# Attention of a hybrid decoder layer: from one head at a time to pairs of heads on the two halves of the array

## What is computed

```python
# stick-breaking head
z = q @ k.T * scale                       # causal: s < t
log_keep = where(causal, -softplus(z), 0)
tail = cumsum(log_keep, reverse=True) - log_keep
a = where(causal, exp(log_sigmoid(z) + tail), 0);  y = a @ v
# MoBA head (own block only)
s = where(t >= s, q @ k.T * scale + bias[bucket(t - s)], -inf);  y = softmax(s) @ v
# layer
h = x + (sigmoid(g_sb) * (y_sb @ w_proj_sb) + sigmoid(g_mb) * (y_mb @ w_proj_moba)) @ w_out
h = h + MoE(rmsnorm(h));  out = rmsnorm(h) * norm_final_g
```

## Time and profile before

| | |
|---|---|
| median of 3 runs | 1309.89 us (1307.11 to 1310.67) |
| span of the profiled execution, first to last instruction | 1304.8 us |
| TensorE busy | 1151.2 us (88%) |
| VectorE, ScalarE, GpSimd busy | 207.3, 210.2, 18.6 us |
| chain that ended last | TensorE 88%, VectorE 7%, ScalarE 4% |
| attention stage, first scores to first L901 | 54.8 to 190.3 us of the span |

### The profile page before, as it was taken

One profiled execution on the slowest core, in us unless ns is written; L12 is line 12 of the kernel. 1 busy time (PEld: TensorE's weight loads), 2 busy tenths in 40 slices (PEclk: granted clock), 3 DMA queues, 4 the chain that ended last, 5 costly groups with the idle time before them and its releaser, 6 DMA issues.

```text
span 1304.8 us, 15767 instructions
## 1 busy us (share of the span) xinstructions
PE 1151.2 (88%) x6100; PEld 472.1 (36%) x6100; DVE 207.3 (16%) x424; ACT 210.2 (16%) x356; POOL 18.6 (1%) x68
## 2 busy tenths in 40 slices
PE   7999999878888888888888888888888888888884
PEld 6675444433333333333333333333333333333331
DVE  1301222231111111111111111111111111111112
ACT  2363230211111111111111111111111111111111
POOL 1010000000000000000000000000000000000000
PEclk9999999979899989999998999899989998999897
DMA  9913324339999999999999999999999999999970
GB/s 336 354 65 129 128 85 160 147 113 386 399 399 397 398 401 393 395 405 401 396 400 395 393 395 395 409 397 387 399 402 397 396 403 403 405 394 399 401 308 33
DMA packets 86624, 437.04 MB, mean 335 GB/s; under 512 B 7704, under 2 KB 7760, under 8 KB 53744
## 3 DMA queue, kind: packets, MB, share of 16 engines
q1 hardware_dynamic: 84880, 434.19, 83.8%
q10 hardware_dynamic: 1424, 1.57, 0.5%
q0 software_dynamic: 304, 1.06, 0.2%
HBM read 435.74 MB, written 1.06 MB: 335 GB/s over the span
## 4 chain that ended last, share of the span: by engine, by line
PE 88%; DVE 7%; ACT 4%; issue 1%; DMA 0%; DVEq 0%; SPq 0%; ACTq 0%
PE bank L984 35%; PE bank L1010 22%; PE bank L818 6%; PE bank L958 5%; PE bank L815 4%; PE bank L949 4%; PE bank L901 2%; PE bank L912 2%; DVE gates L758 2%; DVE gates L760 2%; DVE gates L754 2%; PE bank L1001 2%; ACT gates L545 2%; ACT gates L547 1%; PE bank L978 1%
## 5 line engine op out<-in xcount | busy, mean ns | idle before, releaser
L984 PE MATMUL bank<-ring,gates 128*64 128x512 f32 x2048 | 460.1, 596 | 0.0
L1010 PE MATMUL bank<-ring,gates 128*64 128x512 f32 x1024 | 286.9, 724 | 22.0 <-ACT gates L547 22.0
L984 PEld LDWEIGHTS bank<-ring,gates 128*64 128x64 f32 x2048 | 140.9, 137 | 252.1 <-issue 244.9
L754 DVE TENSOR_SCALAR gates<-bank 128x512 f32<-128x512 f32 x32 | 22.1, 691 | 862.0 <-PE bank L984 862.0
L1010 PEld LDWEIGHTS bank<-ring,gates 128*64 128x64 f32 x1024 | 84.0, 166 | 205.3 <-issue 174.7
L1001 PE MATMUL bank<-ident,gates 128*128 128x128 f32 x128 | 21.1, 289 | 95.9 <-DVE gates L760 95.9
L818 PE MATMUL bank<-ring,colsT 128*128 128x512 f32 x192 | 85.0, 596 | 0.0
L545 ACT ACTIVATE gates<-gates 128x512 f32<-128x512 f32 x32 | 20.1, 629 | 398.7 <-DVE gates L754 398.7
L958 PE MATMUL bank<-gates,scatter_w 64*128 64x512 f32 x264 | 65.6, 615 | 0.7 <-ACT gates L550 0.7
L550 ACT ACTIVATE gates<-bank 128x512 f32<-128x512 f32 x32 | 19.1, 597 | 290.2 <-PE bank L1010 290.2
L949 PEld LDWEIGHTS bank<-onehot,qkT 128*128 128x128 bf16 x1584 | 49.1, 99 | 28.7 <-issue 26.0
(11 more groups left out here) (168 smaller groups left out, 501.2 us busy)
## 6 DMA issues: line engine op xcount, KB each, us to landing
ring<-in_w_gate_up_dram SPq DMA_DIRECT2D x256, 1024.0 KB, 9.0
ring<-in_w_down_dram SPq DMA_DIRECT2D x128, 1024.0 KB, 7.1
ring<-in_w_in_dram SPq DMA_DIRECT2D x10, 2048.0 KB, 18.9
ring<-in_w_out_dram SPq DMA_DIRECT2D x1, 4096.0 KB, 13.7
ring<-in_w_proj_sb_dram SPq DMA_DIRECT2D x1, 2048.0 KB, 7.6
ring<-in_w_proj_moba_dram SPq DMA_DIRECT2D x1, 2048.0 KB, 13.4
resid<-in_x_dram SPq DMA_DIRECT2D x2, 512.0 KB, 3.7
bias<-u_scratch POOLq DMA_DIRECT2D x1, 1024.0 KB, 12.6
```

Of the source, the lines that this page charges most:

```text
L754: V.tensor_scalar(gate_t, bank[4][:, :], SWIGLU_LIMIT, None, ALU.min).then_inc(gate_rd, 1)
L984: ins = mm(bank[4 + i][SLOTS * c:SLOTS * (c + 1), :], xeT[:, k, :], ring[:, k, i * D + c * CH:i * D + (c + 1) * CH], start=False, stop=k = ...
L1010: ins = mm(bank[6][SLOTS * c:SLOTS * (c + 1), :], rows, ring[:, KD + s, j * D + c * CH:j * D + (c + 1) * CH], start=k == 0, stop=k == KD - 1)
```

## The change

Steps go over pairs p = 0 to 7 (0 to 3 stick-breaking, 4 to 7 MoBA), each pair being heads 2p and 2p+1. Queries and keys of a pair lie in rows 0 to 63 and 64 to 127, so its score products are issued in turn for the two row halves of the array, into different banks; its value products go in turn to the two column halves. Score banks are 2, 3, 4 and 7, two pairs of two; values take banks 5 and 6; the transposes of a MoBA head go back into its own score bank. The four `att_` buffers keep their size, so they hold one pair. At step p TensorE runs `scores(p)`, two units, `middle(p-1)`, second units, `mix_values(p-2)`. ScalarE, VectorE and GpSimd go by pairs as well. Lines left out of the diff (removed ones above all) are marked by "...".

```diff
@@ -76,12 +76,14 @@
     first_fill += [("N", c, t) for c in range(6, NCH) for t in range(NT)]
     second_fill = {3: ("N", V_MB, 0), 6: ("N", V_MB, 1)}
     fill_at, second_at = {}, {}
...
+    for p in range(NH // 2):
+        for s in (2 * p, 2 * p + 1):
+            fill_at[s] = len(units)
+            units.append(first_fill[s])
+        for s in (2 * p, 2 * p + 1):
+            if s in second_fill:
+                second_at[s] = len(units)
+                units.append(second_fill[s])
     unit_no = {u: n for n, u in enumerate(units)}
     NU = len(units)
+        z_bank = [bank[2], bank[3], bank[4], bank[7]]
+        o_bank = [bank[5], bank[6]]
+        PAIRS = NH // 2
+        SB_PAIRS = HSB // 2
@@ -390,13 +397,15 @@
                 nc.gpsimd.affine_select(out=diagonal(t), in_=diagonal(t), compare_op=ALU.is_gt, fill=0.0, base=0,
                                         pattern=[[0, 2], [1, P]], channel_multiplier=-1).then_inc(ready, 1)
-            for s in range(HSB + 1):
-                if s < HSB:
-                    pool.wait_ge(softplus, s + 1)
-                    mask(att_s[:, s % 2, :], keep_rd)
-                if s >= 1:
-                    pool.wait_ge(weight_raw, s)
-                    mask(att_w[:, (s - 1) % 2, :], weights_rd)
+            for p in range(SB_PAIRS + 1):
+                for b in range(2):
+                    if p < SB_PAIRS:
+                        pool.wait_ge(softplus, 2 * p + b + 1)
+                        mask(att_s[:, b, :], keep_rd)
+                for b in range(2):
+                    if p >= 1:
+                        pool.wait_ge(weight_raw, 2 * (p - 1) + b + 1)
+                        mask(att_w[:, b, :], weights_rd)
             def experts(done, r):
@@ -467,44 +476,58 @@
             for u in range(lead):
                 evacuate(u)
...
+            def mark(ins):
+                steps[0] += 1
+                ins.then_inc(act_step, 1)
+                return steps[0]
+            for p in range(PAIRS + 1):
+                if p < SB_PAIRS:
+                    act.wait_ge(z_ps, p + 1)
+                    absd = [mark(nc.scalar.activation(att_a[:, b, :], z_bank[(2 * p + b) % 4][:, 0:TRI], ACT.Abs))
+                            for b in range(2)]
+                    if p == 0:
                         act.wait_ge(u_out, 16)
...
+                    if p >= 1:
+                        act.wait_ge(softplus, 2 * p)
+                    small = []
+                    for b in range(2):
+                        act.wait_ge(act_step, absd[b])
+                        small.append(mark(nc.scalar.activation(att_e[:, b, :], att_a[:, b, :], ACT.Exp, scale=-1.0)))
+                    for b in range(2):
+                        act.wait_ge(act_step, small[b])
+                        nc.scalar.activation(att_e[:, b, :], att_e[:, b, :], ACT.Ln, bias=1.0).then_inc(ln_rd, 1)
+                elif p < PAIRS:
+                    for b in range(2):
+                        act.wait_ge(score_rd, 2 * (p - SB_PAIRS) + b + 1)
+                        for q, (c0, c1) in enumerate(((0, P), (P, TRI))):
+                            nc.scalar.activation(att_s[:, b, c0:c1], att_s[:, b, c0:c1], ACT.Exp,
+                                                 bias=nmx[:, b, q:q + 1], accum_out=rs[:, b, q:q + 1]
+                                                 ).then_inc(prob_raw, 1)
+                if p < PAIRS:
+                    evacuate(fill_at[2 * p])
+                    evacuate(fill_at[2 * p + 1])
+                if p >= 1:
+                    act.wait_ge(mid_ps, p)
+                    if p >= 2:
+                        act.wait_ge(pv_ps, p - 1)
+                    for b in range(2):
+                        z = z_bank[(2 * (p - 1) + b) % 4][:, 0:TRI]
+                        if p - 1 < SB_PAIRS:
+                            nc.scalar.activation(att_w[:, b, :], z, ACT.Exp).then_inc(weight_raw, 1)
+                        else:
+                            nc.scalar.activation(att_w[:, b, :], z, ACT.Copy).then_inc(probT_rd, 1)
+                for s in (2 * p, 2 * p + 1):
+                    if s in second_at:
+                        evacuate(second_at[s])
             act.wait_ge(unit_rd, NU)
             for t in range(NT):
                 nc.scalar.activation(gates[:, t, :], gates[:, t, :], ACT.Sigmoid).then_inc(sigm_rd, 1)
...
+            act.wait_ge(pv_ps, PAIRS)
             act.dma_start(bdown_sb, b_down[0]).then_inc(late_in, 16)
@@ -615,36 +638,37 @@
             V.tensor_copy(bgu[2 * E:3 * E, :], gates[2 * E:3 * E, 0, :]).then_inc(piece_d, 1)
             dve.wait_ge(bias_in, 16)
...
+            for p in range(PAIRS + 2):
+                if p < SB_PAIRS:
+                    dve.wait_ge(z_ps, p + 1)
+                    if p >= 1:
+                        dve.wait_ge(mid_ps, p)
+                    for b in range(2):
+                        dve.wait_ge(ln_rd, 2 * p + b + 1)
+                        V.scalar_tensor_tensor(out=att_s[:, b, :], in0=z_bank[(2 * p + b) % 4][:, 0:TRI], scalar=0.0,
+                                               in1=att_e[:, b, :], op0=ALU.max, op1=ALU.add).then_inc(softplus, 1)
+                elif p < PAIRS:
+                    dve.wait_ge(z_ps, p + 1)
+                    dve.wait_ge(mid_ps, p)
+                    for b in range(2):
+                        h = 2 * (p - SB_PAIRS) + b
+                        z = z_bank[(2 * p + b) % 4]
+                        V.tensor_tensor(att_s[:, b, 0:P], z[:, 0:P], bias[:, h, P - 1::-1], ALU.add)
+                        link(V.tensor_tensor(att_s[:, b, P:TRI], z[:, P:TRI], bias[:, h, ::-1], ALU.add))
+                        V.reduce_max(mx[:, b, 0:1], att_s[:, b, 0:P], AX_X)
+                        link(V.reduce_max(mx[:, b, 1:2], att_s[:, b, P:TRI], AX_X))
+                        V.tensor_scalar(nmx[:, b, :], mx[:, b, :], -1.0, None, ALU.mult).then_inc(score_rd, 1)
+                    for b in range(2):
+                        h = 2 * (p - SB_PAIRS) + b
+                        dve.wait_ge(prob_raw, 2 * (h + 1))
+                        link(V.reciprocal(rr[:, b, :], rs[:, b, :]))
+                        for q, (c0, c1) in enumerate(((0, P), (P, TRI))):
+                            V.tensor_scalar(att_s[:, b, c0:c1], att_s[:, b, c0:c1], rr[:, b, q:q + 1], None, ALU.mult
+                                            ).then_inc(prob_rd, 1)
+                if p >= 2:
+                    pair = p - 2
+                    dve.wait_ge(pv_ps, pair + 1)
+                    V.tensor_copy(yT[:, pair, :], o_bank[pair % 2][:, 0:T]).then_inc(pv_rd, 1)
@@ -819,72 +843,86 @@
                                  stop=k == KD - 1)
                 ins.then_inc(unit_ps, 1)
...
+            def scores(p):
+                sticks = p < SB_PAIRS
+                j = p % SB_PAIRS
+                if p == 1:
+                    pe.wait_ge(u_rd, 1)
+                if p >= 2:
+                    if p - 2 < SB_PAIRS:
+                        pe.wait_ge(weight_raw, 2 * (p - 1))
                     else:
...
+                        pe.wait_ge(probT_rd, 2 * (p - 1 - SB_PAIRS))
+                pe.wait_ge(unit_rd, unit_no[("T", K_SB if sticks else K_MB, j)] + 1)
+                for part in range(2):
+                    for b in range(2):
+                        z = z_bank[(2 * p + b) % 4]
+                        r0 = HEAD_DIM * b
+                        q = qkT[r0:r0 + HEAD_DIM, (0 if sticks else 8) + j, :]
+                        k = qkT[r0:r0 + HEAD_DIM, (4 if sticks else 12) + j, :]
+                        if sticks:
+                            if part == 0:
+                                ins = mm(z[:, 0:T], k[:, 0:P], q, start=True, stop=True)
+                            else:
+                                ins = mm(z[:, T:TRI], k[:, P:T], q[:, P:T], start=False, stop=True, skip_group_check=True)
+                        else:
+                            if part == 0:
+                                ins = mm(z[:, 0:P], q[:, 0:P], k[:, 0:P], start=True, stop=True)
+                            else:
+                                ins = mm(z[:, P:TRI], q[:, P:T], k, start=True, stop=True)
+                ins.then_inc(z_ps, 1)
+            def middle(p):
+                for b in range(2):
+                    z = z_bank[(2 * p + b) % 4]
+                    a = att_s[:, b, :]
+                    if p < SB_PAIRS:
+                        pe.wait_ge(keep_rd, 2 * p + b + 1)
+                        mm(z[:, 0:T], neg_tri[:, :], a[:, 0:T], start=False, stop=True, skip_group_check=True)
+                        mm(z[:, P:T], neg_one[:, :], a[:, T:TRI], start=False, stop=True, skip_group_check=True)
+                        ins = mm(z[:, T:TRI], neg_tri[:, :], a[:, T:TRI], start=False, stop=True, skip_group_check=True)
+                    else:
+                        pe.wait_ge(prob_rd, 2 * (2 * (p - SB_PAIRS) + b + 1))
+                        for i in range(3):
```

(68 more changed lines are left out.)

24 lines of the change are left out of this document (removed).

## The result

The changed kernel takes 1333.78 us (median of 4 runs, 1332.09 to 1334.66) against 1308.5 us (4 runs, 1306.81 to 1310.67): ratio 1.0194, 95% interval 1.0176 to 1.0211, 25.3 us slower. The kernel before has executions of two lengths, 1306.3 to 1307.3 (8 of its 31) and 1309.7 to 1311.4, and two of the four behind the 1308.5 are short ones; against the 1310.1 to 1310.3 that is its median in the experiments the loss is 23.4 to 23.6. The forecast was 1327.8, in a range of 1318 to 1337. The time lies in that range, and the loss came through waits and the clock, as forecast, but it was forecast at 17.9, and the time lies above the 1323 to 1332 that the sum was given by itself.

A forecast was written before the change was run, and what follows sets the result against it. TensorE's work was taken to bound the attention stage. Saved work and today's gap against added waits gave +9.9 us, with the clock +17.9: span 1304.8 to 1322.7, median 1327.8 us, range 1318 to 1337.

The forecast's parts named there:

- TensorE work saved: Attention stage: overlapping halves and fewer changes of array shape for pairs save TensorE 12.7 us.
- today's gap: TensorE's waits at the end of the attention stage before the change, some 0.25 us, subtracted in the sum.
- (a): Stick-breaking: scores of pairs 3 and 4 wait for ScalarE's `att_w` writes, 2 x 1.0 = 2.0 us, table load hidden.
- (b): MoBA: `att_s` reuse delays VectorE and ScalarE, so scores of pairs 5, 6 and 7 wait, 3 x 5.1 = 15.3 us.
- (c): End of attention: no scores or units left to cover the last middle and values, waits of 5.5 us.
- (d): Lowered TensorE clock behind the four long gaps, 2.0 us each, 8.0 us; bounds 0 and 11.4.
- rival 3: Deeper loss: each gap costs 2.8 us of clock, or the table load waits too; 1330 to 1333 us; chance 0.10.
- rival 1: Halves do not overlap in so short a run of products: saving 3.6 us, time 1336.9 us; chance 0.13.
- The scatter's 0.56: Share of the serial price, from four products on alternating row halves in the expert loop, taken for pair scores and values.
- Rival 4: VectorE starts a MoBA pair right behind its scores, units covering it: faster, median 1299.2 us; chance 0.03.
- Rival 2: TensorE's clock stays up or nearly so behind the gaps: +10 to +12, 1320 to 1322 us; chance 0.15.

The follow-up runs named there:

- e7: Changed kernel without new buffers, reordered: TensorE runs scores, values, first unit, middle, second unit, and ScalarE's order follows; 1297.2 us, stage 121.95 us.
- e9: As e7, but both heads' value products go into one column half; part of the computation changes against intent; 1300.4 us, stage 127.10 us.
- e10: As e7, but both heads' score products read rows 0 to 63, one row half; 1299.7 us, stage 127.14 us.
- e5: Changed kernel with four `att_s` buffers instead of two, `att_w` keeping two; VectorE waits for an earlier middle; 1307.2 us.
- e3: Changed kernel with four buffers each for `att_s` and `att_w`, the new ones in idle `scaled`; 1297.5 us.
- e2: Changed kernel with two ScalarE wait lines swapped, values waited for first and middle second; 1328.0 us.
- e8: As e3, but all products of a pair's first head are issued ahead of the second's; 1297.2 us, stage 122.13 us.
- e1: Changed kernel with unused full-array products filling TensorE's gaps in steps 2 to 6; 1322.7 us.

## Why the prediction was right, and where it was short

The terms of the sum, as forecast and as the changed kernel's trace gives them:

| term | forecast | measured |
|---|---|---|
| TensorE work saved | -12.7 | -14.2 |
| today's gap | -0.25 | -0.25 |
| (a) two stick-breaking waits | +2.0 | +4.6 |
| (b) three MoBA waits | +15.3 | +14.9 |
| (c) the end | +5.5 | +4.5 |
| (d) clock | +8.0 | +16 |
| sum | +17.9 | +25.6 |

The saved work is 135.45 - 0.25 less the 121.0 that e7 needs (121.95 with one gap of 0.96). The waits are 2 x 2.31, 3 x 4.95 and the gaps at the end, 2.85 + 0.60 + 1.03. The clock is what is left of the stage, 158.74 - 121.0 - 4.6 - 14.9 - 4.5 = 13.7, and 29.95 - 27.68 = 2.3 in the output projection. The sum stands beside a median that moved by 25.3, or by 23.4 to 23.6 against the later medians of the kernel before. It is made from one profiled execution of each kernel, so it is good to some 2 us.

That the range held was partly luck. The measured time lies just above the 1330 to 1333 of rival 3, which had a chance of 0.10, and the range reached that far only for rival 1, which did not come true.

**Saved work.** Right in kind, a little small. A run of four products reaches the full halving: 0.85 and 0.80 a pair, not 0.93 and 0.88. The scatter's 0.56 was no good guide for it. Here the rule of the Trainium skill, "TensorEngine Tiling (Array Packing)", section Theoretical Speedup (up to twice for a side of 64), was the better number, and the trace agrees with it: 1.3 us that I had decided against it. Rival 1, no overlap, is refuted by the chain and by e9 and e10.

**(b) and (c).** Right to 1 us. `scores(p+1)` waited 4.95 where 5.1 was forecast, through just the links named: bias and maximum of both heads, the second head's Exps, both evacuations, both writes. e5 shows that it is `att_s`. Rival 4, an early start of VectorE with `att_w` as it was, is what e5 then built: 1307.2, not the 1299.2 that it was given. Its waits of (a) have the table load and some clock on top, and each MoBA step still waits 1.0 for the writes of `att_w`. e3's 1297.5 is near 1299.2 only because it takes (a) away as well.

**(a), the step that failed.** "The table load before the Exp started at 75.80, before the middle was over at 76.24, so it does not wait with the Exp and stays hidden." The row was right and the conclusion too wide. The Exp has two waits, and the load stands behind the one written last and ahead of the other. Before, the last one (the values of head h-2) had long been met; in the changed kernel it is the one that comes late. e2 shows it by the order alone. This was the second half of rival 3, "the table load stays behind the wait in (a), 2.6", and the measured 4.6 is 2.0 + 2.6.

**(d), mis-sized twice.** "So the waits of (a) should cost nothing more": with the load they became gaps of 2.3 instead of 1.0, and behind them the scores and units took 3.2 and 1.7 more than at full clock (1.23 + 0.43 + 9.50 against 0.85 + 7.10; 0.49 + 0.59 + 15.43 against 0.85 + 13.93). e2's gaps of 1.5 and 1.0 cost nothing, so at 1.0 the sentence would have held. And the gaps of 4.95 cost 2.0 (0.80 + 0.85 + 15.09 against 0.85 + 13.93), 2.3 and 2.5, the end 2.1 in the stage and 2.3 behind it, 11.2 in place of 8.0. Nor could one row have told the price: behind the same gap of 4.05 the 16 transposes that the prediction read at 3.41 took 2.42 in e9, 2.90 in e10, 3.35 in e7 and 3.68 in e8. Rival 2, no clock loss, is refuted by the granted clock of 0.50 behind the gaps; e1 shows what the clock cost.

The prediction also took 5.1 us to lie outside the span. The results now give profiled executions with both numbers (1334.66 with a span of 1333.0), so it is 1.7, and the profiled execution of before was one of its shorter ones. The difference was not touched by that, since it was made against the span.

## What to carry to other kernels

Who joins two steps into one halves the depth of every buffer that is counted in steps: list each "may write when" wait and see where its releaser now stands in the order of work; here that cost more than the overlap gave, and an order with a unit of other work between the release and the next use gave all of it back. Count a gap on TensorE at its length plus what the slower clock takes behind it, here 1.7 to 3.2 us for each gap of 2.3 to 5 us ahead of scores in the changed kernel, and 16 in total against 14.2 of saved work. Give it a range, since in e5 one gap of 2.31 cost nothing. Where an instruction needs a table and has two waits, look which of them the table load stands behind.

## What the runs showed of the hardware that I had not expected

- Two groups of products in different row or column halves overlapped fully when issued one whole group after the other: 0.86 us for the scores of both heads, where alternating issue took 0.85; in one half 1.51 (scores) and 1.45 (values).
- On ScalarE the table load came after the wait written last and before the one written first, in both orders of the two waits (89.03 in the changed kernel, 88.97 and 101.05 in e2).
- A gap of 2.31 us on TensorE was followed by a lowered clock in both places of the changed kernel, with 3.2 and 1.7 us lost; in e5 one such gap lost 1.6 and the other nothing; the gaps of 1.50 and 0.97 in e2 lost nothing. Full-array products without use in the gap kept the granted clock at 1.00.
